# Pooled branch and modulation in pieces beside the first attention's tiles, instead of a stage of their own

## What is computed

```python
# first block
a = dsa_attention(q, k, v, qi, ki, wi, k_sel) * silu(z_a)      # 8 heads, 2 kv heads, 256 selected keys per token
for g, w in enumerate((2, 4, 8, 16)):                          # multiscale_pool, 4 groups of 128 channels
    pooled[g] = trailing_mean(u_b[g], w) - u_b[g]
    mixed[g] = pooled[g] @ pool_w[g]                           # 128 x 128
b = mixed * pool_scale * silu(z_b)
x = x + (g0 * (a @ w_branch_a) + g1 * (b @ w_branch_b)) @ w_out
# second block
ada = silu(c) @ w_ada + b_ada                                  # 1024 -> 3072: shift, scale, gate
h = rms(x, g_pre) * (1 + scale) + shift
...
x = x + gate * rms(y, g_post)
```

## Time and profile before

| | us |
|---|---|
| median of 3 runs (3367.64 to 3369.92) | 3369.39 |
| the profiled execution, its time | 3370.03 |
| its span | 3368.3 |
| TensorE busy, of the span | 3139.5 (93%) |
| VectorE, ScalarE, GpSimd busy | 1735.6 (52%), 1553.7 (46%), 964.5 (29%) |
| mean granted clock of TensorE | 0.961 |
| first attention, first DMA to the pooled stage's first DMA | 1054.21 to 1481.59 |
| pooled stage, first DMA to the output stage's | 1481.59 to 1559.81 |

### The profile page before, as it was taken

How to read it: one execution, slowest core, us unless ns; L and a number is a source line. 1 busy time by engine, 2 the same in 40 slices (tenths; PEclk the granted TensorE clock), 3 DMA queues, 4 the chain that set the end, 5 groups by cost and what they waited for, 6 DMA issues and landing times. The chain is left out here.

```text
span 3368.3 us, 42865 instructions
## 1 busy us (share of the span) xinstructions
PE 3139.5 (93%) x15732; PEld 2546.7 (76%) x15732; DVE 1735.6 (52%) x3611; ACT 1553.7 (46%) x2449; POOL 964.5 (29%) x705
## 2 busy tenths in 40 slices
PE   7995999889996999978999989979999999989998
PEld 7994888667885677745878768867888788868787
DVE  6775799978996666546441166642211131133433
ACT  4544689756983777731110033323544344431111
POOL 3541012100222666621222133322222222212222
PEclk9996999989997999989999989979999999999999
DMA  5666333443334211148652254446343633345522
GB/s 176 203 189 227 91 101 89 117 158 97 100 101 158 66 52 40 40 148 290 158 142 97 93 189 147 144 134 204 111 142 124 208 123 119 125 141 158 140 100 88
DMA packets 434154, 448.92 MB, mean 133 GB/s; under 512 B 30896, under 2 KB 324144, under 8 KB 432304
## 3 DMA queue, kind: packets, MB, share of 16 engines
q1 hardware_dynamic: 433968, 446.47, 42.8%
HBM read 283.61 MB, written 162.79 MB: 133 GB/s over the span
## 5 line engine op out<-in xcount | busy, mean ns | idle before, releaser
L2417 PE MATMUL p_pr<-p_hT,p_w_hi 128*128 128x512 f32 x896 | 355.5, 397 | 16.3 <-DMA p_hT<-s_hT 16.0
L1234 PE MATMUL p_pr<-p_hT,p_w_hi 128*128 128x512 f32 x896 | 355.8, 397 | 13.1 <-POOL p_w_lo L1017 9.6
L1235 PE MATMUL p_pr<-p_hT,p_w_hi 128*128 128x512 f32 x896 | 353.3, 394 | 0.0
L1236 PE MATMUL p_pr<-p_hT,p_w_lo 128*128 128x512 f32 x896 | 353.1, 394 | 0.0
L2418 PE MATMUL p_pr<-p_hT,p_w_hi 128*128 128x512 f32 x896 | 350.7, 391 | 0.0
L2419 PE MATMUL p_pr<-p_hT,p_w_lo 128*128 128x512 f32 x896 | 349.6, 390 | 0.0
L1440 POOL TENSOR_TENSOR a_prob<-a_prob,a_inv 128x1024 f32<-128x1024 f32 (+12 forms) x104 | 250.5, 2419 | 187.6 <-DVE a_inv L1485 187.4
L1057 ACT ACTIVATE p_relu<-p_isc,p_level 128x2048 int8<-128x2048 f32 (+5 forms) x192 | 276.4, 1441 | 21.5 <-DVE p_level L1154 17.2
L1017 POOL TENSOR_TENSOR p_w_lo<-p_w_raw,p_w_hi 128x256 fp32r<-128x256 f32 x144 | 108.0, 781 | 616.8 <-DVE p_level L1154 398.4
L730 PE MATMUL t_pj_ps<-t_w_hi,t_hT_slot 128*128 128x356 f32 (+2 forms) x768 | 271.1, 353 | 10.7 <-DVE t_w_lo L584 6.1
L732 PE MATMUL t_pj_ps<-t_w_hi,t_hT_slot 128*128 128x356 f32 (+2 forms) x768 | 264.1, 344 | 0.0
(11 more groups left out here) (262 smaller groups left out, 6982.4 us busy)
## 6 DMA issues: line engine op xcount, KB each, us to landing
p_w_raw<-in_w_in SPq DMA_DIRECT2D x112, 512.0 KB, 4.3
s_hT<-t_hT_slot SPq DMA_DIRECT2D x32, 1024.0 KB, 6.0
p_hT<-s_hT SPq DMA_DIRECT2D x64, 512.0 KB, 9.8
s_gT<-p_o_sb SPq DMA_DIRECT2D x128, 256.0 KB, 4.9
o_gates<-s_gT SPq DMA_DIRECT2D x64, 512.0 KB, 5.2
s_qT<-t_qT_slot SPq DMA_DIRECT2D x32, 512.0 KB, 2.7
s_zuT<-p_o_sb SPq DMA_DIRECT2D x64, 256.0 KB, 4.9
pl_wada<-in_w_ada SPq DMA_DIRECT2D x6, 2048.0 KB, 19.2
```

The source lines that it names most:

```text
L1234: nc.tensor.matmul(pr[n % NPR][:], wh, hi, start=(k == 0), stop=False)
L1235: nc.tensor.matmul(pr[n % NPR][:], wh, lo, start=False, stop=False)
L1236: last = nc.tensor.matmul(pr[n % NPR][:], wl, hi, start=False, stop=(k == KD - 1))
L2417: nc.tensor.matmul(pr[n % NPR][:], wh, hi, start=(k == 0), stop=False)
```

## The change

- The pooled stage is gone from `PHASES`. Its work stands in the first attention, tied to step numbers.
- Modulation: 12 pieces of 256 columns, at steps 4, 7, ..., 37 (8 matmuls each, L1770 of the new file). Weights come 1 MB at a time, two pieces ahead, into the SBUF space of the last half of the keys; the keys of that half are loaded at steps 41 and 49. VectorE takes a result one step later.
- Pooled branch: 32 pieces of 256 columns, piece x at step 46 + 7x. SP loads u (272 columns with its halo, 256 at a group's start) and z five steps before, VectorE makes sums and mean at the step (L1647 and L1650), TensorE maps two steps later (L1782), VectorE scales and gates four steps later (L1663), SP stores five steps later. There is one buffer for u, two for z, two for sums; the result of the last operation is the matmul's input.
- One PSUM bank (`side`) serves both. For it the values' two banks become one: the first weighing of a turn now waits for the gating of the turn before.
- Weighing groups end at a turn's end: a turn's tiles are cut into the fewest even groups of at most four. Slots for transposed tiles: 7 instead of 8.
- Key loads: the first two quarters at the start, the parameters between them.

```diff
-    NS, NT, NPT, NPROB = 3, 3, 8, 3
+    NS, NT, NPT, NPROB = 3, 3, 7, 3
...
-    o_ps = [ps(f"o_ps{n}", [P, PAIRS * P]) for n in range(2)]
+    o_ps = ps("o_ps", [P, PAIRS * P])
+    side = ps("side", [P, 2 * P])
...
+    def ada_step(n):
+        return 4 + 3 * n
...
+    def pool_step(x):
+        return 46 + 7 * x
...
     def weighed_at(n):
         m = n - LAG
-        size = 2 if m < PAIRED else 4
-        return list(range(m - size + 1, m + 1)) if m >= 0 and m % size == size - 1 else []
+        if not 0 <= m < N_TILES:
+            return []
+        turn, j = TILES[m]
+        tiles = TURNS[turn][0] + 1
+        parts = -(-tiles // 4)
+        ends = [tiles - b * tiles // parts - 1 for b in range(parts + 1)]
+        return list(range(m - (j - ends[ends.index(j) + 1]) + 1, m + 1)) if j in ends[:-1] else []
...
+            def load_ada(n):
+                if n >= 2:
+                    sp.wait_ge(rowed, n - 1)
+                for r in range(2):
+                    sp.dma_start(w_ada[:, 2 * (n % 2) + r, 2 * BANK:].rearrange("p (k n) -> p k n", n=WIDE),
+                                 c.w_ada_2[0, r * BANK:(r + 1) * BANK, n * WIDE:(n + 1) * WIDE].rearrange("(k p) n -> p k n", p=P)
+                                 ).then_inc(ada_loaded[n % 2], 16)
+
+            def load_pool(x):
+                g, j, cols = pool_place(x)
+                sp.wait_ge(halo, g + 1)
+                if x:
+                    sp.wait_ge(pooled_done, x)
...
+            def pool(x):
+                g, j, _ = pool_place(x)
+                width = WINDOWS[g]
+                dve.wait_ge(u_loaded, 16 * (x + 1))
+                if x:
+                    dve.wait_ge(mapped, x)
+                src, span, n = u, 1, 0
+                while span < width:
+
+                    lo = 2 * span - 1
+                    dst = runs[n % 2]
+                    step(nc.vector.tensor_tensor(dst[:, lo:], src[:, lo:], src[:, lo - span:HALO + WIDE - span], ALU.add))
+                    src, span, n = dst, span * 2, n + 1
+                out = pooled_in(g)
+                last = nc.vector.scalar_tensor_tensor(out=out, in0=src[:, HALO:], scalar=1.0 / width, in1=u[:, HALO:],
+                                                      op0=ALU.mult, op1=ALU.subtract)
...
+            def beside(n):
+                for x in at_step(n - 1, ada_step, N_ADA):
+                    take(x)
...
+                for x in at_step(n, pool_step, N_POOL):
+                    pool(x)
...
+                for x in at_step(n - 4, pool_step, N_POOL):
+                    finish_pool(x)
...
-                if j == 0 and turn >= 2:
-                    pe.wait_ge(gated, turn - 1)
+                if j == 0 and turn:
+                    pe.wait_ge(gated, turn)
...
+            def map_pool(x):
+                g, _, _ = pool_place(x)
+                if x == 0:
+                    pe.wait_ge(wp_loaded, 16)
+                    pe.wait_ge(taken, taken_by(N_ADA))
+                else:
+                    pe.wait_ge(out_done, x)
+                pe.wait_ge(pooled_done, x + 1)
+                nc.tensor.matmul(side[:], w_pool[:, g], pooled_in(g), start=True, stop=True).then_inc(mapped, 1)
 
             for n in range(STEPS):
                 if n < N_TILES:
                     for turn, r, m in SCORES_AT[n]:
                         scores(turn, r, m)
                     turn_keys(n)
+                for x in at_step(n, ada_step, N_ADA):
+                    ada(x)
+                for x in at_step(n - 2, pool_step, N_POOL):
+                    map_pool(x)
                 for m in weighed_at(n):
                     weigh(m)
...
-PHASES = ["tok1", "proj1", "att1", "pool", "out1", "tok2", "second", "out2"]
+PHASES = ["tok1", "proj1", "att1", "out1", "tok2", "second", "out2"]
```

More of the change, by code:

```diff
@@ L1318, in phase_attention @@
     LAG = 2
-    PAIRED = 12
     def packed():
@@ L1401, in load_z, with load_keys @@
                              ).then_inc(z_loaded[turn % 2], 16)
-            load(0)
-            loaded = NQ
-            for n in range(4):
+            def load_keys(n):
+                if n:
+                    sp.wait_ge(k_loaded, 16 * n)
+                    sp.wait_ge(v_loaded, 16 * n)
+                if n == 2:
+                    sp.wait_ge(rowed, N_ADA)
                 sp.dma_start(f32(kT[:, :, n * BANK:(n + 1) * BANK]),
@@ L1420, in _ @@
                     loaded += 1
+                for n in range(KEYS[turn] + LAG + 1 if turn else 0, KEYS[turn + 1] + LAG + 1):
+                    beside(n)
                 sp.wait_ge(gated, turn + 1)
@@ L1493, in finish, with take @@
                     dve.wait_ge(stored[s], 16 * (turn // 2))
-                nc.vector.tensor_tensor(aT[:, s].rearrange("p c t -> p (c t)"), o_ps[s][:], z[:, s].rearrange("p c t -> p (c t)"),
+                nc.vector.tensor_tensor(aT[:, s].rearrange("p c t -> p (c t)"), o_ps[:], z[:, s].rearrange("p c t -> p (c t)"),
                                         ALU.mult).then_inc(gated, 1)
+            step = Counter(dve, chain)
+            def take(n):
+                dve.wait_ge(rowed, n + 1)
+                if n == N_COLS:
+                    dve.wait_ge(g_loaded, 16 * 4)
+                for j in range(2 if n < N_COLS else 0):
+                    if n or j:
+                        dve.wait_ge(taken, taken_by(n) + j)
+                    nc.vector.tensor_tensor_reduce(out=unread[:], in0=side[:, j * P:(j + 1) * P], in1=c.ident[:], scale=1.0,
+                                                   scalar=0.0, op0=ALU.mult, op1=ALU.add,
+                                                   accum_out=col[:, 2 * n + j:2 * n + j + 1]).then_inc(taken, 1)
+                if n >= N_COLS:
+                    part = gate_b[:, (n - N_COLS) * WIDE:(n - N_COLS + 1) * WIDE]
+                    nc.vector.tensor_tensor(part, side[:], part, ALU.add).then_inc(taken, 1)
@@ new lines, in clear_halo @@
+            def clear_halo(g):
+                if g:
+                    dve.wait_ge(pooled_done, g * SEQ // WIDE)
+                else:
+                    dve.wait_ge(combined, 1)
+                nc.vector.memset(u[:, 0:HALO], 0.0).then_inc(halo, 1)
+            def pool(x):
[13 more added lines that the diff above has]
+                                                      op0=ALU.mult, op1=ALU.subtract)
+                if j == 0:
+                    step(last)
+                    step(nc.vector.tensor_tensor(out[:, 0:width], src[:, HALO:HALO + width], c.rcount[:, g, 0:width], ALU.mult))
+                    last = nc.vector.tensor_tensor(out[:, 0:width], out[:, 0:width], u[:, HALO:HALO + width], ALU.subtract)
+                last.then_inc(pooled_done, 1)
```

277 lines of the change are left out of this document (111 added, 166 removed).

## The result

The changed kernel takes 3409.47 us in the median of its runs (3406.38 to 3410.6), the kernel before 3368.61 beside it: 1.0112 times as long, 95% interval 1.0099 to 1.0125, so slower by 41 us. I had forecast slower, by 14, and a range that ended at 3400.

The account below looks back on a forecast made before the run. TensorE's own instruction list was taken to bound the attention. The sum 3370.0 - 78.2 + 41.7 + 17.0 + 3 - 6 + 3 + 30 + 3 gave 3383.5, on the median's footing 3383 us; range over all 3350 to 3400.

Parts of the forecast that it names:

- The mechanism: First attention: GpSimd's normalisations hold VectorE's pooled SBUF operations until they end, and TensorE stops for the map; +30 us.
- The term for the tile's waits: TensorE's waits for pooled tiles: ten pieces 19 us, fourteen 8 us, eight 3 us; together +30, bounds +5 and +55.
- The fixed terms: Attention without waits and clock: modulation +41.7, pooled map +17.0, weighings +3, gaps filled -6, start +3 us.
- The gaps: TensorE's idle and low-clock time from about 1086 to 1113 us, filled by modulation: -6 us, bounds 0 and -7.
- The groups and the bank: TensorE's weighings: 80 groups instead of 71, +3 us, bounds 1 and 5; one bank costs nothing in the steady part.
- its 0.53: Pooled map on TensorE: 32 matmuls, 64 records at 0.215 us, plus 0.1 per entry; +17.0 us for both.
- The attention's own VectorE work is not touched, since L1460 reads PSUM: First attention: VectorE's operation reading PSUM, 687 ns mean, is not held by GpSimd; no term in the sum.
- rival C: Much slower: GpSimd takes its turn between a chain's VectorE operations, so scores wait too; +20, 3403 us, chance 0.07.
- The term for the clock: TensorE's low clock after stalls as long as the one near 1104 us, and late negations: +3 us, bounds 0 and +10.
- A (faster): Pieces find VectorE free and unheld, or TensorE's distance is longer; map waits 5, clock 0, 3355 us; chance 0.29.
- B (the same, waits of 15): No difference: same mechanism, but normalisation remainders half as long; waits 15, 3366 us; chance 0.19.
- D: Modulation weights arrive late, the third piece behind some 9 MB of other loads; wait of 10 us, 3393 us, chance 0.05.

Follow-up runs that it names:

- with a PSUM operand: Changed kernel with each piece cut to one operation on 256 columns, its first input from PSUM instead of SBUF: 3353.08 us, beside 3368.49 for the kernel before.
- the better version: Changed kernel with pieces moved by a table to steps where GpSimd is idle, ahead of reciprocals, map four steps later, 19 table entries changed again: 3351.92 us against 3369.15.
- later map: Changed kernel with TensorE mapping a piece four steps after VectorE makes it instead of two, finish and store two steps later too: 3385.77 us, ratio 1.0051.
- moved, behind: Changed kernel with pieces moved by table to steps where GpSimd's queue is empty, but behind the reciprocals, map two steps later: 3427.86 us, ratio 1.0174.
- ahead: Changed kernel at its own steps, with each piece ahead of its step's reciprocal on VectorE instead of behind: 3381.74 us, ratio 1.0041.
- moved, without and with the later map: Changed kernel, pieces at steps where GpSimd's queue is empty, ahead of reciprocals: 3368.43 us with the map two steps later, 3357.99 with it four steps later.
- no normalisations: Changed kernel with GpSimd's normalisations cut to one column each, waits and signals kept: 3355.74 us against 3369.86 for the kernel before, ratio 0.9957.

## Why the prediction was right and wrong

**The mechanism was right.** It was forecast as the deciding term, and the runs without normalisations, with the order turned, and with a PSUM operand each show it in another way. The Trainium skill ("SBUF — State Buffer", section "SBUF: two separate sides") speaks of an exclusive lock, held for a whole instruction against a GpSimd instruction, by VectorE operations with two SBUF inputs or in a two-port mode. The timelines agree that the whole instruction is waited out, and put numbers to its edges, which are smaller than the full length of the one held: the held operation of 0.42 us ends 0.28 us behind GpSimd, that of 0.29 us 0.15 behind, and the normalisation that started 0.26 us before the sum ended, at step 151, lost 0.12.

**The term for the tile's waits was right in size**: +30 us in the sum, 29.9 in the waits. Its parts were not, and that they add up is luck: the ten pieces behind a reciprocal of their own step cost 14.4 us instead of 19, among other things since a piece's first operation gets in ahead of GpSimd (0.42 us in the timeline of step 151), and the other 22 cost 15.7 instead of 11. Of these 3.6 fall on the piece of step 249, which meets a whole normalisation, since on VectorE nothing stands between it and the reciprocal of an earlier step. VectorE's work was right too: 49 us for chains, 49.9 by the five groups of the better version (102.0 in the changed kernel, so 52 us of it are holding).

**The fixed terms were right together.** Without the two terms for waits and clock, the sum adds 41.7 + 17 + 3 - 6 + 3 = 58.7 us to the attention. The better version has the same work with next to no waits, and its attention lasts 485.1 us, 57.7 more than before. One by one they differ: the modulation's twelve pieces of 16 records hold TensorE 3.27 to 3.65 us each, 41.0 together, as forecast. The gaps gave about 4 us instead of 6: from 1083 to 1133 us TensorE is idle 1.7 us instead of 3.9, at a clock of 0.97 instead of 0.93. The 8.4 us ahead of transposes lie before step 4, where the modulation starts. The groups and the bank made a difference of 1 us, within the noise, instead of 3. A map seems to cost less than its 0.53: at one place of the better version (1228 us) its first record starts 0.25 us before the score behind it.

**What failed is the step "The attention's own VectorE work is not touched, since L1460 reads PSUM" and what it left out of the sum.** The operations are indeed as long as before, but they stand behind the held ones in VectorE's program. With three score banks TensorE can be three scores ahead and then waits: 11.0 us, and no term of mine held it. I had asked who waits for the piece, not who waits for what stands behind it on VectorE. The rival C had such a wait, but under a condition (GpSimd taking turns inside a chain) that it doesn't need. The run with the later map shows that this is a way of its own: with the tile's wait nearly gone, this one doubles.

**The term for the clock was mis-sized**, +3 with a bound of 10. From 1083 us to the end of the stage:

```profile
1083.00:1594.27 511.27, 466.16 (x3020) 339.34 (x3016) 345.64 (x1123) 295.94 (x494) 247.42 (x101) 0.97 0.29 88
```

and in the better version:

```profile
1083.00:1538.17 455.17, 448.74 (x3023) 333.07 (x3021) 294.52 (x1123) 294.31 (x494) 245.94 (x101) 1.00 0.32 99
```

A mean of 0.97 over 511 us is about 15 us of progress less, 1.00 none. I had measured the price of one stall (1.7 us for the one near 1104) and took two of that size for the whole program. The stalls come in several places. In the changed kernel, around the one of 4.2 us at 1509 to 1514:

```profile
1500.00:1510.00 10.00, 9.18 (x60) 6.79 (x60) 8.28 (x28) 7.21 (x11) 4.88 (x2) 1.00 0.13 42
1510.00:1520.00 10.00, 5.94 (x23) 3.18 (x24) 5.36 (x11) 2.59 (x3) 2.23 (x1) 0.66 0.12 27
```

Part of the second window is at 1.2 GHz instead of 2.4. Over the versions the mean clock from 1083 us on follows the waits (tile and scores together): 53.9 us of waits at 0.95 (moved, behind), 40.9 at 0.97 (the change), 25.2 and 23.9 at 0.98 (ahead, later map), 15.9 and 7.6 at 0.99 (moved, without and with the later map), 10.7 and 2.1 at 1.00 (no normalisations, the better version).

So 56.7 us stand above the fixed terms (114.4 - 57.7), where the sum had 33: 30 for the tile, 9 ahead of scores (11.0 less the 2.1 that the better version has), at most about 15 for the clock, since a low clock costs nothing while TensorE waits; that makes up to 54, and the rest stays open. The later stages' 4.5 us aren't explained by the change: from the output stage's first matmul to the end the kernels of this case take between 1800 and 1808 us, with the program there unchanged.

**The rivals.** A (faster) fell with the holding, B (the same, waits of 15) with its size, D with the waits: none for the modulation's weights. C's time, 3403, came closest. What it describes occurs once in the changed kernel: at step 95 two normalisations are queued, the sum takes 1.26 us and the operation behind it 2.64, with GpSimd's second normalisation between; TensorE waits 1.0 us for that tile. The waits ahead of scores come at other pieces.

## What to carry to other kernels

Before work is put on VectorE beside GpSimd, ask of each operation where its operands lie, and of each place whether GpSimd has just been released. Of the places tried here, the best for SBUF work on VectorE was directly ahead of the instruction that releases GpSimd, at steps where GpSimd's queue is empty, and the worst directly behind it: the same pieces at the same steps were 59 us apart. Of a delay on an in-order engine count two things, who waits for the delayed result and who waits for whatever stands behind it, and add the lower clock that goes with it where TensorE is the one that waits: here 41 us of waiting went with some 15 us of lost clock.

## What was not expected of the hardware

An operation of VectorE with a single SBUF input and its output in SBUF (scaling 256 float32 columns, 0.29 us free) was held by GpSimd to the end of its normalisation as one with two inputs was, up to 2.90 us. With one operand in PSUM and one in SBUF it took 0.43 at most, at the same steps. The Trainium skill's two-port mode, in the section named above, would cover this case; that the operation ran in such a mode is not shown by a run here, only that it is faster when free than the one with two inputs (0.29 against 0.42) and is held.
